# Building the neighbourhood-attention bias on the chip from its small table, in a three-block transformer kernel on one Trainium2 core

## The reference, cut to what matters

```python
# query at grid (row qr, column qc), key at (kr, kc), head h, layer l
start = clip(qc - 8, 0, 64 - 16)
inside = start <= kc < start + 16
bias[l, h, q, k] = na_rpb[l, h, kr - qr + 7, kc - qc + 15] if inside else -1e30
scores = q @ k.T * 64 ** -0.5 + bias       # then softmax over the keys
```

## Time and profile before

| what | value |
|---|---|
| runs | 1529.57, 1530.85, 1532.55 us (median 1530.85) |
| the profiled execution | 1529.57 us, of which the traced span is 1527.6 us |
| granted TensorE clock, mean | 0.981 |
| busy share: TensorE matmul, weight load, VectorE, ScalarE, GpSimd | 95%, 81%, 59%, 44%, 2% |
| DMA | 235.84 MB, 154 GB/s on average |
| chain of work that ended last | TensorE 85%, VectorE 5%, ScalarE 5%, DMA 3% |

### The profile page before, as it was taken

How to read it: one execution, slowest core, us unless ns; L and a number is a source line. 1 busy time by engine, 2 the same in 40 slices (tenths; PEclk the granted TensorE clock), 3 DMA queues, 4 the chain that set the end, 5 groups by cost and what they waited for, 6 DMA issues and landing times.

```text
span 1527.6 us, 23465 instructions
## 1 busy us (share of the span) xinstructions
PE 1451.2 (95%) x9372; PEld 1242.4 (81%) x9372; DVE 906.2 (59%) x1390; ACT 677.7 (44%) x1080; POOL 36.9 (2%) x53
## 2 busy tenths in 40 slices
PE   5999999999999999999988899998999999899998
PEld 2787656888888888889846799997999999698996
DVE  1677545564242424478645555657898545786867
ACT  3421345553140313464244644555344554664644
POOL 0000000000000000000060000000000000000000
PEclk9999999999999999999999899998999999899999
DMA  9322485032231304155274454463454444354553
GB/s 381 131 83 81 166 332 221 1 139 83 110 110 72 121 27 165 55 172 190 83 302 167 164 194 154 177 221 138 166 169 167 162 139 138 138 176 183 192 188 116
DMA packets 33126, 235.84 MB, mean 154 GB/s; under 512 B 3664, under 2 KB 3664, under 8 KB 5264
## 3 DMA queue, kind: packets, MB, share of 16 engines
q1 hardware_dynamic: 31936, 228.31, 41.2%
q0 software_dynamic: 1104, 6.29, 1.2%
HBM read 233.54 MB, written 1.05 MB: 154 GB/s over the span
## 4 chain that ended last, share of the span: by engine, by line
PE 85%; DVE 5%; ACT 5%; DMA 3%; issue 1%; SPq 0%; ACTq 0%
PE ps L525 45%; PE ps L571 21%; PE ps L545 5%; PE ps L680 2%; DMA w<-in_stream 2%; PE ps L809 1%; PE ps L627 1%; DMA C<-in_consts 1%; DVE w_lo L432 1%; ACT w_hi L422 1%; PE ps L599 1%; PE ps L842 1%; PE ps L814 1%; PE ps L826 1%; PE ps L719 1%
## 5 line engine op out<-in xcount | busy, mean ns | idle before, releaser
L525 PE MATMUL ps<-h_hi,w_hi 128*128 128x256 f32 (+1 forms) x1568 | 494.2, 315 | 4.6 <-DVE h_lo L1710 2.8
L525 PE MATMUL ps<-h_lo,w_hi 128*128 128x256 f32 (+1 forms) x1568 | 489.4, 312 | 0.0
L525 PE MATMUL ps<-h_hi,w_lo 128*128 128x256 f32 (+1 forms) x1568 | 489.2, 312 | 0.0
L422 ACT ACTIVATE w_hi<-w 128x1024 fp32r<-128x1024 f32 x332 | 332.6, 1053 | 245.6 <-DMA w<-in_stream 245.5
L432 DVE TENSOR_TENSOR w_lo<-w,w_hi 128x1024 fp32r<-128x1024 f32 x332 | 390.5, 1219 | 79.4 <-ACT w_hi L422 74.9
L525 PEld LDWEIGHTS ps<-h_hi,w_hi 128*128 128x128 f32 x1568 | 302.3, 193 | 25.0 <-issue 5.7
L525 PEld LDWEIGHTS ps<-h_lo,w_hi 128*128 128x128 f32 x1568 | 302.4, 193 | 16.3 <-issue 0.5
L525 PEld LDWEIGHTS ps<-h_hi,w_lo 128*128 128x128 f32 x1568 | 302.1, 193 | 15.9
L571 PE MATMUL ps<-w_hi,g_hi 128*128 128x512 f32 x472 | 185.1, 392 | 1.7 <-DVE g_lo L2068 0.9
L571 PE MATMUL ps<-w_lo,g_hi 128*128 128x512 f32 x472 | 183.8, 389 | 0.0
L571 PE MATMUL ps<-w_hi,g_lo 128*128 128x512 f32 x472 | 183.7, 389 | 0.0
(11 more groups left out here) (254 smaller groups left out, 1657.4 us busy)
## 6 DMA issues: line engine op xcount, KB each, us to landing
w<-in_stream SPq DMA_DIRECT2D x214, 1024.0 KB, 4.9
U<-in_bias POOLq DMA_DIRECT2D x2, 1024.0 KB, 5.3
SW<-in_small POOLq DMA_DIRECT2D x2, 896.0 KB, 6.7
X<-in_x SPq DMA_DIRECT2D x1, 1024.0 KB, 13.2
X<-in_ctx SPq DMA_DIRECT2D x1, 1024.0 KB, 15.3
X<-in_masks POOLq DMA_DIRECT2D x1, 1024.0 KB, 8.2
GA<-in_gpost POOLq DMA_DIRECT2D x2, 512.0 KB, 4.5
out<-X SPq DMA_DIRECT2D x2, 512.0 KB, 2.6
```

Of the source, the lines that this page charges most:

```text
L422: act.activation(k.w_hi[:, c.slot, half], k.w[:, c.slot, half], ACT.Copy).then_inc(k.hi_done, 1)
L525: last = pe.matmul(k.banks(2 * c.pair, n, j * (512 if tiles == 2 else n)), w[a][:, c.slot, at:at + 128], h[b][:, kt * stride:kt * stride + n],
```

## The change

The host no longer spreads the bias. It passes `na_rpb` as 8 rows of 465 numbers (15 by 31, one row for each layer and head) and one mask `window`, 128 by 256. The chip then:

- at the start (layer 0, before the small weights) copies each row 64 times in HBM, 8 DMAs into `rpb_rows` of shape (8, 64, 465), and waits for all of them (`rpb_out`);
- in each layer, after the features are complete, gathers the bias with 16 DMAs. Each writes 64 partitions by 4 by 64 numbers: the rows of `rpb_rows` are read with a step one shorter than a row, so that query column qc reads from a start shifted by qc. Every contiguous piece of it is 64 numbers, 256 bytes;
- loads `window` into columns 9728 to 9983 of `U`, which `qr` also uses, waits for all 17 DMAs, and adds the window to the bias with one GpSimd `tensor_tensor` of 128 by 2048 (semaphore `bias`);
- in layer 1 issues the load of `masks2` only behind this wait and add.

VectorE's wait for the bias moves from the first na unit to before the write of `qr` after chunk `sc_c`, since the window lies where `qr` is written. Its four small clears of the convolution borders become two clears of the whole buffers, 1144 and 1032 columns.

```diff
+RPB = 15 * 31
-... "bias_in": 16, ...
+... "bias_in": 17 * 16, ...
-                        ("qr", 9728, 512), ("sc_in", 10240, 1032), ("cf_acc", 11328, 1024),
+                        ("qr", 9728, 512), ("window", 9728, 256), ("sc_in", 10240, 1032), ("cf_acc", 11328, 1024),
     def zeros():
         dve.wait_ge(k.s("h", f"mix{l}"), h_count(f"mix{l}", 4, KT - 1))
-        for ends in (slice(0, 15), slice(271, 286)):
-            o.then(dve.memset(cf_in[:, :, 0:seg, ends], 0.0))
-        for ends in (slice(0, 1), slice(257, 258)):
-            last = o.then(dve.memset(sc_in[:, :, 0:seg, ends], 0.0))
-        o.wait(last)
+        o.then(dve.memset(b["cf_in"], 0.0))
+        o.link(dve.memset(b["sc_in"], 0.0))
...
             k.wait(dve, "mla_mm", l, 1)
+            k.wait(dve, "bias", l, 1)
             dve.tensor_scalar(b["qr"][:, 0:nq], k.banks(7, nq), MLA_SCALE, None, ALU.mult).then_inc(k.s("qr"), 1)
...
         if kind == "na" and q0 == 0:
-            k.wait(dve, "bias_in", l, 16)
...
             pool.wait_ge(k.chunk_mm, FIRST["win", 0])
+            for hd in range(DEPTH * HEADS):
+                pool.dma_start(t["rpb_rows"][hd], rows(t["rpb"][hd], GRID)).then_inc(k.s("rpb_out"), 16)
         pool.dma_start(k.SW[:, :], t["small"][l]).then_inc(k.s("small_in"), 16)
+        pool.wait_ge(k.s("rpb_out"), 16 * DEPTH * HEADS)
...
-        pool.dma_start(b["bias"], t["bias"][l]).then_inc(k.s("bias_in"), 16)
+        for hd in range(HEADS):
+            for r in range(4):
+                at = ((l * HEADS + hd) * GRID) * RPB + (7 - r) * 31 + 15
+                src = bass.AP(t["rpb_rows"].tensor, at, [[RPB - 1, GRID], [31, 4], [1, GRID]])
+                dst = b["bias"][64 * (r % 2):64 * (r % 2) + 64, hd * 512 + (r // 2) * 256:hd * 512 + (r // 2) * 256 + 256]
+                pool.dma_start(dst.rearrange("p (i n) -> p i n", i=4), src).then_inc(k.s("bias_in"), 16)
+        pool.dma_start(b["window"], t["window"]).then_inc(k.s("bias_in"), 16)
+        k.wait(pool, "bias_in", l, 17 * 16)
+        bias = b["bias"].rearrange("p (m n) -> p m n", m=8)
+        pool.tensor_tensor(bias, bias, b["window"].unsqueeze(1).broadcast_to([128, 8, 256]),
+                           ALU.add).then_inc(k.s("bias"), 1)
```

More of the change, by code:

```diff
@@ L269 @@
 SMALL_N = 2 * 384 + 512 + 512
-FIRST_LAYER = {"small_in": 16, "bias_in": 16, "latent_sq": 2, "mla_mm": 4, "mla_in": 2, "cf_act": 2, "cf_tanh": 2, "cf_hi": 2, "cf_var": 2, "sc_y": 2, "hidden": 16, "squared": 16}
+FIRST_LAYER = {"small_in": 16, "bias_in": 17 * 16, "latent_sq": 2, "mla_mm": 4, "mla_in": 2, "cf_act": 2, "cf_tanh": 2, "cf_hi": 2, "cf_var": 2, "sc_y": 2, "hidden": 16, "squared": 16}
 FIRST_LAYER.update({step: 16 for step in ("scores", "nmax", "exp", "p", "pt_mm", "pt_act", "pt_dve", "o_mm")})
@@ L2509, in shape_constants @@
     c[:, C_SIGN], c[:, C_SIGN + 1] = np.where(p // 32 % 2, -1, 1), np.where(p // 64, -1, 1)
+    qc, kc = p % GRID, np.arange(256) % GRID
+    start = np.clip(qc - 8, 0, GRID - 16)[:, None]
+    window = np.where((kc >= start) & (kc < start + 16), 0, MASKED).astype(np.float32)
     q = (p[:, None] + np.array([0, 128]))[:, :, None, None]
@@ L2516, in shape_constants @@
     masks2[:, :A_WIDTH + sum(B_WIDTHS)] = np.concatenate(parts, axis=1)
[L2517 to L2531, removed]
+    return c, window, masks2
 def kernel(**inputs):
@@ L2538 @@
     a = {name: np.asarray(v) for name, v in inputs.items()}
-    consts, masks2 = shape_constants()
+    consts, window, masks2 = shape_constants()
     arrays = {
         "x": a["x"], "ctx": a["ctx"], "feats": feature_vectors(a), "small": small_weights(a),
-        "bias": band_bias(a["na_rpb"]), "lam": a["diff_lambda_2"].reshape(-1),
+        "rpb": a["na_rpb"].reshape(DEPTH * HEADS, RPB), "lam": a["diff_lambda_2"].reshape(-1),
         "gpost": np.stack([a["post_mix_g_2"][0], a["post_ffn_g_2"][0]]),
-        "pos": a["positions_2"], "consts": consts, "masks2": masks2,
+        "pos": a["positions_2"], "consts": consts, "window": window, "masks2": masks2,
         "stream": weight_stream(a),
@@ L2551 @@
         t[name] = nc.dram_tensor(f"in_{name}", v.shape, mybir.dt.from_np(v.dtype), kind="ExternalInput").ap()
+    t["rpb_rows"] = nc.dram_tensor("rpb_rows", (DEPTH * HEADS, GRID, RPB), f32, kind="Internal").ap()
     t["out"] = nc.dram_tensor("out", (1, SEQ, D), f32, kind="ExternalOutput").ap()
```

## The result

The changed kernel takes 1540.08 us (median of 6 runs, 1536.11 to 1541.33) against 1530.21 us for the kernel before in the same measurement: 9.9 us or 0.6% slower, ratio 1.006 with a 95% interval of 1.0046 to 1.0076. The profiled execution took 1539.73 us with a span of 1537.9, 10.3 us longer than the span before.

A forecast was written before the change was run, and what follows sets the result against it. TensorE, busy 95% of the span, was taken to bound the kernel. All terms were hidden and summed to 0, so the profiled 1529.6 us stood, 1.3 under the median: forecast 1531.0 us, range 1528.5 to 1546.

The forecast's parts named there:

- rival A: Gathers' small DMA pieces are dear, delaying layer 1's bias and a weight load: 1531 to 1549 us, chance 0.20.
- B: Issuing the gathers on GpSimd is dear, 2.1 to 3 us each, bias late: 1532 to 1548 us, chance 0.10.
- Does the add block VectorE?: GpSimd's add beside VectorE's two-input SBUF instructions: from one overlap in the trace, no blocking, nothing charged.
- Rival C: GpSimd's add holds VectorE for 4.7 us from about 708 in layer 1: 1531 to 1533 us, chance 0.04.
- VectorE's 2.43 us of idling before the reciprocal: Layer 1, before 709.38: idle time taken as cover for the larger clears and a VectorE block.
- the deadline of 727.2: Layer 1: latest start of the `qr` write before TensorE loses time, 41.4 us behind the bias chain's start.
- The issue of a gather: GpSimd's queue: 1.07 us taken per gather, 17.1 for 16; 0.53 if independent of pieces, 2.1 as outer bound.
- the 0.04 taken: DMA engine time per 256-byte gather piece in us, a quarter of the 4 KB packet; called the softest number.
- the prediction's other estimate of 5: Moving a layer's gathers, pieces counted as 512 bytes by the Trainium skill: 2 MB, 5 us.
- the 1 and 1.3 us in rival A's sum: Two terms added, without explanation, to layer 1's bias-ready time beside gather moving, weight loads and the 4.7 us add.
- The sum had the bias ready at 712.9: Layer 1: start 685.8 plus issuing 17.1, window 0.5, landing 4.8 and add 4.7; 7.5 us before VectorE's wait.
- D: Faster, if TensorE waited on the old bias transfer; price 0, a luckier clock gives 1527 to 1528 us, chance 0.04.

The follow-up runs named there:

- one_input: Changed kernel with GpSimd's add replaced by a one-input multiply by 1 of 1280 columns, mask left out: 1537.21 us, ratio 1.0043.
- no_add: Changed kernel without GpSimd's add of the window, VectorE waiting for the 17 DMAs instead: 1531.82 us, ratio 1.0002 to the kernel before.
- small_clears: Changed kernel with the four small VectorE clears of the kernel before: 1534.69 us, ratio 1.0028.
- add_in_8: Changed kernel with GpSimd's add split into 8 instructions of 128x256: 1538.77 us, ratio 1.0053.

## Why the prediction was right or wrong

The forecast, 1531.0 us and no change, was wrong, and so was the working behind it. The range held the time by luck: 1540.1 lies in the middle of what was given to rival A, and neither A nor B happened.

**The step that failed** is "Does the add block VectorE?", where the prediction says that "nothing is charged". It set one overlap above the Trainium skill ("SBUF — State Buffer", "Who interferes with whom"), which says that a VectorE instruction with two SBUF inputs and a GpSimd instruction that reads SBUF exclude each other for a whole instruction, and that one that only writes does not. The runs agree with the Trainium skill on all three points: 3.8 us held behind a two-input add, 2.15 behind a one-input multiply, none behind clears. The row showed too little: VectorE started at 765.71, 0.33 us ahead of the recorded end of the GpSimd instruction. In one_input the taps were released 2.15 us behind 702.13, at 704.3, 0.6 us ahead of the recorded end at 704.92; in the changed kernel it was 0.2 us. An instruction's last few tenths can already be free, so a start there proves nothing.

**Rival C was the case, at the wrong price.** It had 4.7 us of block (3.8 measured) and a time of 1531 to 1533. Its cover was misread: I took VectorE's 2.43 us of idling before the reciprocal and the deadline of 727.2. Idle time says when VectorE has nothing to do, not who needs what it did earlier. The first demand on VectorE in this stretch is the copy of `q`, with 1.6 us of slack. Rival A names this very path, `q` at 704.52 and the sums at 707.36, but asks only what a late weight load would do to it. Then the clears were costed at nothing under the same 2.43 us, as if no other delay used it: 2.1 and 3.8 have 1.6 us in common. And the price of a wait of TensorE was taken as its length; the clock behind it added 3.3 us in the first profile.

**The other terms.** The issue of a gather is 0.61 us, against 1.07 taken and 0.53 as the lower bound: 256 pieces cost GpSimd little more than 128. In 687 to 696 GpSimd's queue moved 0.98 MB in 47.8% of 16 x 9 us:

```profile
q0 software_dynamic: 476, 0.98, 47.8%
```

which is 0.018 us for 256 bytes, below the 0.04 taken and far from rival A's 0.095, and 4.6 us on 16 engines for the 4096 pieces of a layer, near the prediction's other estimate of 5; the weight load beside the gathers landed in 5.6 us, where it took 7.7 beside the old bias load. From the issue of the window to the start of the add it was 2.3 us (4.8 taken; the 1 and 1.3 us in rival A's sum stood on no row). The add alone is 4.6 us (4.7). The sum had the bias ready at 712.9; it was ready at 706.0 even with the add held. VectorE's moved wait held nothing: line 1894 was released by TensorE, 0.61 us of idling, as the earlier trace rows show it. The copies in HBM took 4.17 us of issue (4.3) and did not delay the gathers of layer 0. The clears took 1.93 us and some 0.3 between them (2.1 to 2.3). Rivals B and D did not occur.

## What to carry to other kernels

Work moved to GpSimd that reads SBUF can cost VectorE nearly its own length (3.8 us of 4.6 here) where VectorE runs instructions with two SBUF inputs; put it where VectorE idles or reads PSUM, and do not count on splitting it. When a delay is hidden under slack, find the first consumer of each result that becomes late, and let all delays of one engine in that stretch draw on one account. A short wait of a busy TensorE can cost more than its length: in these profiles the lower clock behind it added 1.8 us to waits of 0.55 and 2.8 us (no_add, one_input), and 3.3 us to waits of 2.2 and 4.3 us (small_clears, the changed kernel).

## What the runs showed of the hardware

GpSimd's DMA issue hardly depends on the number of pieces here: 0.52 us for 64 rows (8 in 4.17 us), 0.53 to 0.68 for 128 rows, 0.61 for 64 x 4 pieces of 256 bytes (16 in 9.77 us). A wait of TensorE of 0.55 us was already followed by a lower clock: the 24 matmuls behind it took 4.25 us instead of 2.98 in no_add. Beside GpSimd's eight short adds each of seven two-input VectorE instructions took 0.5 us longer, whether it was 0.47 or 1.22 us long by itself (add_in_8).
